# Dense gate/up products with the activations stationary and 512 weight columns moving

## The reference, cut to what matters

```
def swiglu(h, w_gu, w_down):                    # w_gu 1024 x 6144, w_down 3072 x 1024
    g, u = jnp.split(h @ w_gu, 2, axis=-1)
    return (jax.nn.silu(g) * u) @ w_down

mod = c_act @ ada_w[l] + ada_b[l]               # one row times 1024 x 6144, for each layer
```

## Time and profile before

| | us |
|---|---|
| runs: lowest, median, highest of 3 | 1333.50, 1334.57, 1335.28 |
| span of the profiled execution | 1330.8 |
| PE busy in it | 1294.8 |
| DVE busy | 577.2 |
| ACT busy | 267.4 |
| dense stage, first to last of its matmuls | 142.25 to 359.7 |

### The profile page before, as it was taken

The page is one execution under the profiler, slowest core; times in us unless marked ns, Lnnn a source line. Parts: engine busy times, 40 slices in busy tenths (PEclk is TensorE's granted clock), DMA queues, the critical chain, the costliest instruction groups (busy, mean ns, idle before and its releaser), DMA issues.

```text
span 1330.8 us, 27861 instructions
## 1 busy us (share of the span) xinstructions
PE 1294.8 (97%) x12266; PEld 810.1 (61%) x12267; DVE 577.2 (43%) x932; ACT 267.4 (20%) x496; POOL 13.0 (1%) x42
## 2 busy tenths in 40 slices
PE   7999899999998999999999999999999999999986
PEld 3888799999844763366345366456545355636622
DVE  2695998888766541232214033132122230422331
ACT  3572444444345540001001001000100000100000
POOL 1000000000000011000000000000000000000000
PEclk9999999999999999999999999999999999999999
DMA  9999758898954269999999999999999999999994
GB/s 353 353 385 338 239 203 310 319 316 312 388 214 162 90 254 399 380 357 418 418 418 418 419 419 419 418 418 418 418 418 418 418 418 419 418 419 418 419 418 198
DMA packets 129436, 477.62 MB, mean 359 GB/s; under 512 B 9408, under 2 KB 36256, under 8 KB 129312
## 3 DMA queue, kind: packets, MB, share of 16 engines
q1 hardware_dynamic: 129008, 475.23, 90.9%
q10 hardware_dynamic: 304, 0.57, 0.1%
HBM read 474.72 MB, written 1.05 MB: 357 GB/s over the span
## 4 chain that ended last, share of the span: by engine, by line
PE 90%; DMA 3%; SPq 3%; ACT 1%; DVE 1%; issue 1%; POOL 0%; ACTq 0%; POOLq 0%; DVEq 0%
PE psum L2077 36%; PE psum L2097 16%; PE psum L1816 5%; PE psum L1817 5%; PE psum L1818 5%; PE psum L1732 4%; SPq L667 3%; PE psum L1881 2%; PE psum L1938 2%; PE psum L1770 2%; PE psum L2055 2%; PE psum L2063 2%; DMA ring<-in_m_w_down 2%; DMA ring<-in_m_w_gu 2%; PE psum L1625 1%; PE psum L1632 1%
## 5 line engine op out<-in xcount | busy, mean ns | idle before, releaser
L2077 PE MATMUL psum<-ring,xe 128*32 128x448 f32 x4704 | 451.5, 539 | 1.4 <-DMA ring<-in_m_w_gu 1.4
L2077 PEld LDWEIGHTS psum<-ring,xe 128*32 128x32 f32 x4704 | 190.2, 110 | 252.0 <-issue 246.6
L2097 PE MATMUL psum<-ring,hT 128*32 128x256 f32 (+1 forms) x3180 | 247.6, 460 | 5.9 <-DMA ring<-in_m_w_down 5.7
L2097 PEld LDWEIGHTS psum<-ring,hT 128*32 128x32 f32 x3180 | 151.0, 110 | 95.8 <-issue 27.2
L1478 DVE TENSOR_TENSOR hs<-sg,psum 128x1344 f32<-128x1344 f32 x10 | 15.5, 1554 | 313.3 <-PE psum L2077 313.3
L1816 PE MATMUL psum<-fh,dhi 128*128 128x256 f32 x384 | 109.9, 286 | 3.7 <-DVE fl L1285 2.5
L1493 DVE STREAM_TRANSPOSE hT<-hs 32x448 f32<-32x448 f32 x120 | 111.8, 943 | 1.6
L1817 PE MATMUL psum<-fl,dhi 128*128 128x256 f32 x384 | 108.7, 283 | 0.0
L1818 PE MATMUL psum<-fh,dlo 128*128 128x256 f32 x384 | 108.6, 283 | 0.0
L864 ACT ACTIVATE dhi<-ring 128x1024 fp32r<-128x1024 f32 x72 | 75.9, 1060 | 90.9 <-PE psum L1818 86.1
L1251 DVE TENSOR_TENSOR dlo<-ring,dhi 128x1024 fp32r<-128x1024 f32 x72 | 88.2, 1225 | 6.9 <-ACT dhi L864 4.7
(11 more groups left out here) (298 smaller groups left out, 1196.3 us busy)
## 6 DMA issues: line engine op xcount, KB each, us to landing
ring<-in_m_w_gu SPq DMA_DIRECT2D x224, 896.0 KB, 23.2
ring<-in_m_w_down SPq DMA_DIRECT2D x118, 896.0 KB, 23.5
ring<-in_ada_w SPq DMA_DIRECT2D x24, 2048.0 KB, 16.1
ring_more<-in_m_w_gu SPq DMA_DIRECT2D x32, 896.0 KB, 22.6
ring<-in_f_w_gu SPq DMA_DIRECT2D x24, 1024.0 KB, 14.3
ring<-in_f_w_down SPq DMA_DIRECT2D x6, 2048.0 KB, 14.7
ring_more<-in_m_w_down SPq DMA_DIRECT2D x10, 896.0 KB, 24.5
ring<-in_a_w_in SPq DMA_DIRECT2D x4, 2048.0 KB, 19.5
```

Of the source, the lines that this page charges most:

```text
L2077: ins = mm(banks[TB * g:TB * g + TB, seg, 0:SEG], block(n), w[:, c0:c0 + SEG], start=first, stop=last, skip_group_check=True)
L2097: ins = mm(y_banks[TB * g:TB * g + TB, o0 + 256 * part:o0 + 256 * part + size], hT[:, t % 2, i, TB * b:TB * b + TB], raw(at // SW)[:, at % ...
```

## The change

1. Gate/up products: for each chunk the 128 tokens of a block are stationary (`fh` or `fl`) and the step's 512 weight columns (256 gate, 256 up) are moving. 6 matmuls of 128x512 a chunk, 48 a pair, 576 in all. The result stands in bank 0 (tokens 0 to 127) and 1 (tokens 128 to 255), with the token over partitions. Silu and the product read and write the same sizes as before.
2. The gated product therefore has to be turned before the down products: `turn_hid` transposes its four 128x128 blocks into bank 3, at step (t,0) for pair t-1, and for the last pair at step (11,4). ACT's rounding and DVE's rest read bank 3 and stand at part 3 of the next pair in place of part 1.
3. Bank 3 is no longer free for modulation sums, so these use the two halves of bank 2. Each vector's sum is issued at the step in which it is complete and turned at the next step; before, the sums stood at the next part 3 and were turned two steps later. A sum now waits for the DVE's `ada` of the vector just before it; before, of the one before that.

```diff
+        def turn_hid(t):
+            pe.wait_ge(hid_done, t + 1)
+            after(pe, gl_ready, t)
+            for i in range(2):
+                for n in range(NB):
+                    last = transposed(hid_bank[:, i, n * P:(n + 1) * P], silu[:, n, i * P:(i + 1) * P], ident[:, :])
+            last.then_inc(hid_turned, 1)
+
+        def moving_split(o, x, w, start, stop):
+            hi, lo = dhi[:, w[0], w[1]:w[1] + 4 * P], dlo[:, w[0], w[1]:w[1] + 4 * P]
+            mm(o, x[0], hi, start=start, stop=False)
+            mm(o, x[0], lo, start=False, stop=False)
+            return mm(o, x[1], hi, start=False, stop=stop)
         for n, (t, part) in enumerate(dense_steps):
             if part == 0 and t:
-                pe.wait_ge(hid_done, t)
+                turn_hid(t - 1)
+            if t == PAIRS_DENSE - 1 and part == 4:
+                turn_hid(t)
...
-                    for c in range(4):
-                        half, i = c // 2, c % 2
-                        last = stationary_split(bank[i][:, SEQ * half:SEQ * (half + 1)], (n % WB, 512 * a + P * c),
-                                                (fh[:, k, :], fl[:, k, :]), k == 0 and half == 0, k == KC - 1)
+                    for b in range(NB):
+                        last = moving_split(bank[b][:, :], (fh[:, k, b * P:(b + 1) * P], fl[:, k, b * P:(b + 1) * P]),
+                                            (n % WB, 512 * a), k == 0, k == KC - 1)
...
-            if (part == 1 and t) or (m == PAIRS_DENSE - 1 and part == 4):
-                act.wait_ge(hid_done, m + 1)
-                nc.scalar.activation(gh[:, m % 2, :, :], silu[:, :, :], ACT.Copy).then_inc(gh_ready, 1)
+            if (part == 3 and t) or (m == PAIRS_DENSE - 1 and part == 4):
+                act.wait_ge(hid_turned, m + 1)
+                nc.scalar.activation(gh[:, m % 2, :, :], hid_bank, ACT.Copy).then_inc(gh_ready, 1)
...
+            for n in range(DSTEPS - 2 - WB):
+                for v, k in ada_ops_beside(n):
+                    if k == KC - 1:
+                        sum_at[v], turn_at[v] = n, n + 1
...
-            pe.wait_ge(ada_done, v - 1)
+            pe.wait_ge(ada_done, v)
```

More of the change, by code:

```diff
@@ L273, in build @@
         hid_done = sem("hid_done")
+        hid_turned = sem("hid_turned")
         gh_ready = sem("gh_ready")
@@ L448, in ada_ops_beside @@
             return [(10 + m // KC, m % KC) for m in range(ops * n // DSTEPS, ops * (n + 1) // DSTEPS)]
-        def ada_summed_by(t):
-            return [v for n, (p, _) in enumerate(dense_steps) for v, k in ada_ops_beside(n)
-                    if k == KC - 1 and dense_pair_time(n) == t]
         def ada_events():
             sum_at, turn_at = {}, {}
[L459 to L462, removed]
+            for n in range(DSTEPS - 2 - WB):
+                for v, k in ada_ops_beside(n):
+                    if k == KC - 1:
+                        sum_at[v], turn_at[v] = n, n + 1
             return sum_at, turn_at
-        def dense_pair_time(n):
-            return next((dense_steps[m][0] for m in range(n + 1, DSTEPS) if dense_steps[m][1] == 0), PAIRS_DENSE)
         def ada_beside(t):
@@ L605, in build @@
         ada_bank = lambda v: bank[2 + v % 2]
+        late_sums = lambda v: bank[2][:, 2 * P * (v % 2):2 * P * (v % 2) + 2 * P]
+        hid_bank = bank[3].rearrange("p (i n) -> p i n", i=2)
         row_bank = lambda v: bank[6 + v % 2]
@@ L805, in ada_copy @@
                     act.wait_ge(ada_mm, v)
-                nc.scalar.activation(sums[:, :], bank[2 + v % 2][:, 0:P], ACT.Copy).then_inc(ada_rowed, 1)
+                nc.scalar.activation(sums[:, :], late_sums(v)[:, 0:P], ACT.Copy).then_inc(ada_rowed, 1)
             def first_tap(T):
@@ L881, in _ @@
                     act.wait_ge(dense_used, dense_steps.index((m, 3)) + 1)
-                    after(act, gl_ready, m)
+                    after(act, hid_turned, m)
                     for i in range(2):
-                        nc.scalar.activation(silu[:, i, :], bank[i][:, 0:SEQ], ACT.Silu).then_inc(silu_done, 1)
-                if (part == 1 and t) or (m == PAIRS_DENSE - 1 and part == 4):
-                    act.wait_ge(hid_done, m + 1)
-                    nc.scalar.activation(gh[:, m % 2, :, :], silu[:, :, :], ACT.Copy).then_inc(gh_ready, 1)
+                        nc.scalar.activation(silu[:, i, :], bank[i][:, 0:2 * P], ACT.Silu).then_inc(silu_done, 1)
+                if (part == 3 and t) or (m == PAIRS_DENSE - 1 and part == 4):
+                    act.wait_ge(hid_turned, m + 1)
+                    nc.scalar.activation(gh[:, m % 2, :, :], hid_bank, ACT.Copy).then_inc(gh_ready, 1)
             for v in range(10, 10 + ADA_IN_DENSE):
@@ L1129, in ada @@
                 if v in TURNED:
-                    total = bank[2 + v % 2][:, P:2 * P].rearrange("p (j m) -> p j m", m=32)[:, :, 0]
+                    total = late_sums(v)[:, P:2 * P].rearrange("p (j m) -> p j m", m=32)[:, :, 0]
                 then(v_.tensor_tensor(mod[:, 4 * v:4 * v + 4], total, cols[:, 4 * v:4 * v + 4], ALU.add), ad)
@@ L1294, in _ @@
                         dve.wait_ge(silu_done, 2 * m + i + 1)
-                        ins = v_.tensor_tensor(silu[:, i, :], silu[:, i, :], bank[i][:, SEQ:2 * SEQ], ALU.mult)
+                        ins = v_.tensor_tensor(silu[:, i, :], silu[:, i, :], bank[i][:, 2 * P:4 * P], ALU.mult)
                     ins.then_inc(hid_done, 1)
-                if (part == 1 and t) or (m == PAIRS_DENSE - 1 and part == 4):
+                if (part == 3 and t) or (m == PAIRS_DENSE - 1 and part == 4):
                     dve.wait_ge(gh_ready, m + 1)
-                    v_.tensor_tensor(gl[:, m % 2, :, :], silu[:, :, :], gh[:, m % 2, :, :].bitcast(F32),
+                    v_.tensor_tensor(gl[:, m % 2, :, :], hid_bank, gh[:, m % 2, :, :].bitcast(F32),
                                      ALU.subtract).then_inc(gl_ready, 1)
@@ L1694, in ada_sums @@
             def ada_sums(v):
-                pe.wait_ge(ada_done, v - 1)
+                pe.wait_ge(ada_done, v)
                 pe.wait_ge(ada_sum, ada_sum_at(v))
                 for j in range(4):
-                    last = mm(bank[2 + v % 2][32 * j:32 * j + 32, 0:P], ones[:, 0:32],
+                    last = mm(late_sums(v)[32 * j:32 * j + 32, 0:P], ones[:, 0:32],
                               ada_acc(v)[:, j * P:(j + 1) * P], start=True, stop=True)
@@ L1705, in ada_turn @@
                 pe.wait_ge(ada_rowed, v - 9)
-                transposed(bank[2 + v % 2][:, P:2 * P], sums[:, :], ident[:, :]).then_inc(ada_mm, 1)
+                transposed(late_sums(v)[:, P:2 * P], sums[:, :], ident[:, :]).then_inc(ada_mm, 1)
             stats(0)
```

## The result

The changed kernel takes 1339.93 us (median of 6 runs, 1338.03 to 1345.20) against 1334.68 for the kernel before. The ratio is 1.0043, with a 95% interval of 1.0025 to 1.0062. It is slower by 5.7 us, where I had forecast 6.5 us faster. Its profiled execution has a span of 1338.3 us, 7.5 more than the earlier trace rows. That overstates the loss: 1338.3 is an ordinary span for the changed kernel (median of its six 1338.05), while 1330.8 is among the shortest of the kernel before (72 later executions: 1330.2 to 1338.7, medians of 1332.4 to 1333.2). So the 3.8 us between median and span are not all outside the span, as I had taken them: in these executions of the kernel before the time is 2.5 us (median) above the span of the same execution.

What follows compares the result with a forecast made beforehand. PE was taken to bound the dense stage, with DVE close behind at 90%. The terms -13.8 + 5.2 + 0.4 + 1.7 = -6.5 us took 1334.6 to 1328.1 us, range 1325 to 1336.

Steps and rivals of the forecast that it cites:

- Gate/up products: Dense stage: 1152 matmuls at 120 ns become 576 at 216 ns, -13.8 us (from -14.4 to 0).
- the loads explain the 120: Gate/up matmuls: 120 ns is one weight load per matmul, not 256 columns' streaming; 512 columns would cover the load.
- rival B: Gate/up matmuls: a fixed 11 to 13 ns each whatever the size, 227 ns for 512 columns; 1334.4 us, chance 0.08.
- rival A: Gate/up matmuls: the 120 ns are the columns' own, so 512 columns take 240 ns; 1341.9 us, chance 0.10.
- The sums in bank 2: Modulation sums sharing bank 2 with a tighter wait for DVE: no cost, with little to spare.
- D: Rival for the dense stage: DVE or a modulation wait becomes the bound, 5 us lost; 1333 us, chance 0.09.
- The transposes: Turning the gated product: twelve groups of four transposes at 0.43 us, +5.2 us (4.2 to 13.0).
- Rival C: Turning the gated product: each transpose takes 0.27 us, +13.0 us in all; 1335.9 us, chance 0.03.
- The end of the stage: Last pair: PE waits for the last transpose, ACT's copy and DVE's subtraction before its down steps, +1.7 us.
- The start: Pair 0: gate/up ends 1.15 us earlier, but DVE lets the product begin only 0.75 us earlier, +0.4 us.
- Who is next: Dense stage after the change: the bound stays with PE, with DVE at 93%.
- Reaches the end: Behind the dense stage: its earlier end starts the expert loads earlier, so all of the gain reaches the program's end.

Runs made afterwards that it cites:

- e4: The changed kernel with 84 unused fp32r matmuls of several sizes added ahead of step 1 of the dense stage; one execution, 1351.98 us.
- e3: The changed kernel with each 512-column gate/up matmul issued as two of 256 columns; 1350.7 us, ratio 1.0096 to the kernel before.
- e8: The changed kernel with 19 idle matmuls where PE waits ahead of the sum of vector 24; 1342.23 us, ratio 1.0052 to the kernel before.
- e1: The changed kernel with late vectors 23 and 24 in two banks again, without the tighter wait; 1334.97 us, ratio 0.9995 to the kernel before.
- e7: The kernel before with only the change's modulation sums, but late vectors 23 and 24 in two banks with the old wait; 1335.64 us, ratio 1.0001.
- e2: The kernel before with only the third part of the change, the modulation sums in bank 2; 1342.27 us, ratio 1.0048.
- e5: e1 with each of the 12 groups of four transposes issued twice; 1342.8 us, ratio 1.0049 to the kernel before.
- e6: e1 with the last pair's product turned one step earlier, between the down steps of pair 10; 1335.87 us, ratio 0.9988 to the kernel before.
- e9: e6 with ten more idle matmuls ahead of the dense stage; 1333.01 us, ratio 0.9979 to the kernel before.
- e10: The kernel before with ten more idle matmuls ahead of the dense stage; 1335.09 us, ratio 0.9992.

## Why the prediction was wrong

**"Gate/up products: -13.8 us" was mis-sized: the pace was 227 to 228 ns, which is -6.7 to -7.7.** The step that failed is "the loads explain the 120". They don't: 120 ns is 107 for the columns and 13 that come with each fp32r matmul of 128 stationary columns, from 256 columns up (e4, e3). In pair 0 the pace is 227 ns, -7.7 us by my sum. Over the whole stage of e8 the 526 distances between gate/up matmuls with nothing else between them average 228.2 ns, against 119.9 for 1123 such distances before: -6.7 us. I had this as rival B at 0.08, with its 227 ns and its 1334.4 us, and e1 came out at 1335.0. The measured 1339.9 is near rival A's 1341.9, but by chance: A's 240 ns are not there, and the loss comes from elsewhere.

What misled me was that the floor of an uncovered load, 113 ns, lies so near 120 that one row seemed to explain the other. A row that is near is not the same mechanism: a load floor of 112 cannot make 120. The loads' starts follow the matmuls' starts in either case and decide nothing. My lower bound had a wrong reading in it too: the K/V products are 16 fp32 matmuls of 512 columns in the kernel and 32 records in the earlier trace rows, so the 429 ns are one of two records of a matmul and say nothing of an fp32r matmul; the 216 ns had only the bf16 row for them. The page "TensorE: Matmul & The Clock Gate" of the Trainium skill, section Back-to-back issue gap, has columns over 2.4 GHz plus 2.5 ns; that is 216 ns for 512. By this rule the trace agrees for bf16 (217) and does not for fp32r (227).

**"The sums in bank 2: nothing" was wrong by the whole loss.** I went through the 13 sums inside the stage, and for these it was right (e7). I left out vectors 23 and 24, which the same function sums behind the stage. There the add that is waited for is not five steps ahead in DVE's list but behind reciprocal and four multiplications of the norm. The wait of 4.3 us stands on the chain, since the K/V products are behind it in PE's list (e1, e2), and the clock falls during it (1.9 us in the trace). By the ratios, 1.0043 - 0.9995, the late wait with what it brings is 0.48%, 6.4 us; e2 alone gives the same, and the traces give 6.3. This was no rival of mine: D looked for a modulation wait in the stage.

**The transposes: right.** Forecast 0.43 a group and 5.2 in all, measured 0.44 and 5.3 (e5). Rival C's 0.27 us is the length of a record, and so are the 275 ns that the prediction cites from the page "TensorE: Matmul & The Clock Gate" of the Trainium skill, Part 4: PE-mode transpose; the pace here is 109 ns (eight in 0.85 us, e5).

**The end of the stage: right.** Forecast 1.7 us, measured 1.7 (e6). **The start:** a loss of 0.4 was forecast, and there was none. From the stage's first matmul to the end of the wait for pair 0's silu product it is 13.01 us before and 12.42 us in e8, which both had no fall of the clock there. The 0.59 us between them is the whole of what pair 0's matmuls had become shorter. The loss hung on the 1.15 us that were mis-sized above.

**The stage's sum.** With what was measured: -6.7 + 5.3 + 0 + 1.7 = +0.3. In executions that both had the fall at the start the stage is 218.85 (after) against 218.70 (e7), +0.2. In two that had none it is 217.37 (e8, whose stage is that of the changed kernel) against 217.19 (before), +0.2 again. The window of e8's start:

```profile
140.00:147.00 7.00, 4.53 (x21) 3.71 (x21) 6.86 (x17) 2.20 (x6) 0.00 (x0) 1.00 1.09 362
```

So the stage came out level where I had -6.5, and the late wait of 6.3 us, for which I had nothing, made the kernel slower.

**Who is next: right.** PE has no wait for `dlo`, with DVE busy for 54.0 of 60 us. **Reaches the end: right.** From the K/V products on, the profiled executions of before, after and e1 need 960.2, 959.3 and 959.4 us, so the 6.3 us reach the end.

## What to carry to other kernels

When a wait is made one step tighter, list every caller of the function that holds it, also those outside the loop that one is looking at, and ask for each what stands in the waited engine's list ahead of the release. When two rows would explain a pace equally well, find the row that tells them apart, or give both real weight; here a distance could be split in columns and a fixed part only by a second width, and none was in the trace. A layout change that saves a small cost on each product and pays with transposes should be summed first with the smallest saving that the rows allow.

## What the runs showed of the hardware

- An fp32r matmul with 128 stationary columns costs 0.417 ns a column and about 13 ns more (227 to 230, 174, 120 ns for 512, 384, 256 columns), and 111 to 112 ns for 128 or 64 columns (medians, e4). With 64 or 32 stationary columns 256 moving ones take 113 ns. A plain fp32 matmul stands in the trace as two records, each some 2.5 ns over two cycles a column (216 ns for 256 columns, 429 for 512).
- Four fp32 transposes of 128x128 between fp32r matmuls cost 0.44 us, the changes of format included (e5, and the changed kernel at 228.53 us).
- A rest of PE of 2.5 us behind 2.6 us of idle matmuls was followed by a fall of the granted clock at the stage's start in eight of the ten profiled executions with that rest; it cost 1.6 us of stage (217.26 in e6 against 215.68 in e9).
- A similar fall in attention comes in some executions and not in others of nearly the same program: the windows from 430 to 444 us have a clock of 0.76 (e7) and 1.00 (e1), with 64 and 86 matmuls. It is worth more than the one at the stage's start. From the K/V products to the end the five profiled executions with a clock of 1.00 from 430 to 470 us (before, after, e1, e4, e9) need 959.3 to 960.6 us, the seven with less (e2, e3, e5 to e8, e10) 963.4 to 965.4. The matmuls of the earlier trace rows begin 108.0 us behind the K/V products in the five and 109.4 to 110.8 in the seven.
- The runs of the kernel before are spread over 8.6 us (1332.5 to 1341.1). That these falls are the reason is likely by the point above; what decides whether one comes was not tested.
